# A decoder layer's expert activations: gates and transposed lists of a token tile made in the last step of the tile in front

## What is computed

```python
s = jnp.einsum('thpd,hpkd->thpk', q, subkeys)
s_top, i_top = lax.top_k(s, 16)                       # per half
cand = s_top[:, :, 0, :, None] + s_top[:, :, 1, None, :]
g_s, g_i = lax.top_k(cand, 16)
e = jnp.take_along_axis(cand_idx, g_i, axis=-1)
g = jax.nn.softmax(g_s, axis=-1)
act = jax.nn.gelu(jnp.einsum('thed,td->the', u[e], xb))
y = jnp.einsum('the,thed->td', g * act, v[e])
```

## Time and profile before

| what | value |
|---|---|
| median of the runs shown | 2279.5 us |
| profiled execution | 2279.13 us, its span 2277.4 us |
| mean granted TensorE clock | 0.944 |
| busy: PE, DVE, ACT, POOL | 2058.1, 1646.1, 854.5, 983.0 us |
| column products begin, units begin, last column | 993, 1093, 1715 us |
| ScalarE's conversion of a column (L2336), mean | 1.051 us |

### The profile page before, as it was taken

How to read it: one execution, slowest core, us unless ns; L and a number is a source line. 1 busy time by engine, 2 the same in 40 slices (tenths; PEclk the granted TensorE clock), 3 DMA queues, 4 the chain that set the end, 5 groups by cost and what they waited for, 6 DMA issues and landing times.

```text
span 2277.4 us, 32421 instructions
## 1 busy us (share of the span) xinstructions
PE 2058.1 (90%) x10515; PEld 1660.1 (73%) x10515; DVE 1646.1 (72%) x2982; ACT 854.5 (38%) x1715; POOL 983.0 (43%) x855
## 2 busy tenths in 40 slices
PE   8998998678789879999899799969987999999997
PEld 7774576334346548889898699969986888888885
DVE  3563156865223434898899999998867889989988
ACT  1232021223202211134766476648753333333331
POOL 1000133333100000047788778967994455554440
PEclk9999899879899879999999999989999999999998
DMA  5333222998740222336798798878999999999992
GB/s 195 79 72 118 90 87 76 363 331 305 263 172 3 111 84 65 98 125 230 233 308 294 232 300 293 292 256 274 308 355 382 373 387 402 405 394 387 385 387 112
DMA packets 239937, 547.81 MB, mean 241 GB/s; under 512 B 22190, under 2 KB 122335, under 8 KB 238394
## 3 DMA queue, kind: packets, MB, share of 16 engines
q1 hardware_dynamic: 110714, 287.40, 35.8%
q0 software_dynamic: 60736, 208.40, 24.9%
q10 hardware_dynamic: 68352, 50.34, 6.7%
HBM read 485.58 MB, written 60.02 MB: 240 GB/s over the span
## 4 chain that ended last, share of the span: by engine, by line
PE 30%; DVE 21%; POOL 5%; issue 4%; DMA 2%; ACT 0%; SPq 0%; DVEq 0%; ACTq 0%; POOLq 0%
PE psum L2797 20%; DVE u_gather L2430 8%; PE psum L2082 5%; PE psum L2551 4%; DVE hT L2458 4%; POOL uL L2196 3%; POOL u_gather L2188 2%; DMA S<-activation_table 2%; DVE eq L1987 1%; PE psum L2073 1%; DVE vL L2739 1%; DVE eq L1990 1%; DVE cand L1965 1%; DVE i_first L1951 0%; DVE vecs L1991 0%
## 5 line engine op out<-in xcount | busy, mean ns | idle before, releaser
L2188 POOL DMA_INDIRECT u_gather<-in_u_rows,gather_ids x160 | 211.3, 1321 | 456.4 <-DVE gather_ids L1998 348.1
L2196 POOL TENSOR_TENSOR uL<-u_raw,uH 128x512 fp32r<-128x512 f32 x256 | 379.3, 1505 | 61.5 <-ACT uH L2114 36.2
L2551 PE MATMUL psum<-hH,uH 128*128 128x384 f32 x1024 | 357.2, 349 | 42.3 <-POOL uL L2196 42.2
L2551 PE MATMUL psum<-hH,uL 128*128 128x384 f32 x1024 | 348.5, 340 | 0.0
L2551 PE MATMUL psum<-hL,uH 128*128 128x384 f32 x1024 | 348.1, 340 | 0.0
L2659 POOL DMA_INDIRECT v_gather<-in_v_rows,idx_now x160 | 236.1, 1476 | 249.5 <-DVE y_sample L2748 153.0
L2430 DVE CUSTOM_DVE_ANT_0 u_gather<-u_gather,h 128x1024 f32<-128x1024 f32 x160 | 292.0, 1825 | 44.9 <-DMA u_gather<-in_u_rows,gather_ids 36.1
L2797 PE MATMUL psum<-vH,wH 128*128 128x512 f32 x768 | 301.6, 393 | 14.8 <-DVE wL L2741 14.7
L2797 PE MATMUL psum<-vH,wL 128*128 128x512 f32 x768 | 300.7, 392 | 0.0
L2797 PE MATMUL psum<-vL,wH 128*128 128x512 f32 x768 | 300.5, 391 | 0.0
L2551 PEld LDWEIGHTS psum<-hH,uH 128*128 128x128 f32 x1024 | 197.0, 192 | 50.6 <-POOL uL L2196 50.3
(11 more groups left out here) (503 smaller groups left out, 3454.9 us busy)
## 6 DMA issues: line engine op xcount, KB each, us to landing
u_raw<-in_uT SPq DMA_DIRECT2D x128, 512.0 KB
S<-in_v_rows SPq DMA_DIRECT2D x64, 512.0 KB
v_rest<-in_v_rows SPq DMA_DIRECT2D x64, 512.0 KB
activation_table<-acts ACTq DMA_DIRECT2D x128, 192.0 KB
gate_table<-Gtile ACTq DMA_DIRECT2D x48, 512.0 KB
S<-gate_table SPq DMA_DIRECT2D x16, 768.0 KB
S<-activation_table SPq DMA_DIRECT2D x16, 768.0 KB
G_rest<-gate_table SPq DMA_DIRECT2D x16, 768.0 KB
```

Source lines behind the costliest of these rows:

```text
L2188: c.nc.gpsimd.indirect_dma_start(c.ug[:, k % RG], None, c.A["u_rows"].rearrange("j i d -> (j i) d"), bass.IndirectOffsetOnAxis(ap=c.ids[:, ...
L2196: ins = c.nc.gpsimd.tensor_tensor(c.uL[:, n % RU, d], c.u[:, n % RAW, d], c.uH[:, n % RU, d].bitcast(F32), ALU.subtract)
L2551: ins = nc.tensor.matmul(column[n % 4][:, 0:ND], w[:, n % RU, d], x[:, d], start=m == 0, stop=m == len(parts) - 1)
```

## The change

For each tile after the first, `tile_pre` runs at the start of the last step of the tile in front, the exponential and the gates in that step's places 0 and 2, and the transposes (`slots_out`, split off `slots_in`) in place 3. ScalarE's three copies (`slots_in`) run at place 0 of the tile's step 0, and the units and routing parts of step 0 are taken in turn with columns and dots like those of the other steps. The routing of a tile is spread over 28 of the 32 slots (34 parts), that of tile 0 over 26 (17 parts). Two of the dot lists change, with the same sums. Transposes wait for the copies of the tile before, and the copies for the comparisons and gatings of the tile before, since both now come sooner.

```diff
--- before.py
+++ after.py
@@ -2152,7 +2152,7 @@
 TSTEP = P // (UNIT * U_STEP)
 LEAD = 4
 STEP_COLS = ((2, 1) * 4, (5, 5, 5, 5, 5, 5, 4, 4), (5,) * 8, (4, 3) * 4)
-STEP_DOTS = ((1, 1, 1, 0, 0, 2, 2, 2), (6,) * 7 + (5,), (7, 6, 6, 6) * 2, (6,) * 8)
+STEP_DOTS = ((1, 1, 1, 0, 0, 2, 2, 2), (6,) * 5 + (5, 5, 7), (6,) * 7 + (8,), (6,) * 8)
 TAIL_DOTS = (2, 1, 1, 1, 1, 0)
 RAW = 3
 RU = 4
@@ -2233,7 +2233,7 @@
             return c.res0[:, 2] if p == 0 else b.res[:, 2] if p < STILE else c.resS[:, 2]
-        def steps(columns, dot, tile_pre, gates_out, tile_gates, slots_in, unit, route, flush):
+        def steps(columns, dot, tile_pre, gates_out, tile_gates, slots_out, slots_in, unit, route, flush):
@@ -2244,9 +2244,11 @@
             for p in range(STILE):
                 for st in range(TSTEP):
                     nc_, nd = STEP_COLS[p][st], STEP_DOTS[p][st]
-                    routed, gates = st == (0 if p else 5), st == (0 if p else 7)
-                    if routed:
-                        tile_pre(p)
+                    next_tile = st == TSTEP - 1 and p + 1 < STILE
+                    if p == 0 and st == 5:
+                        tile_pre(0)
+                    if next_tile:
+                        tile_pre(p + 1)
                     for i in range(max(U_STEP, nc_, nd)):
                         if i < nc_:
                             columns(n)
@@ -2254,21 +2256,22 @@
                         if i < nd:
                             dot(k)
                             k += 1
-                        if routed and i == 0:
-                            gates_out(p)
-                        if gates and i == 1:
-                            tile_gates(p)
-                        if st == 0 and i == 4 and p:
+                        if p == 0 and (st, i) == (5, 0):
+                            gates_out(0)
+                        if p == 0 and (st, i) == (6, 1):
+                            tile_gates(0)
+                        if next_tile and i == 0:
+                            gates_out(p + 1)
+                        if next_tile and i == 2:
+                            tile_gates(p + 1)
+                        if next_tile and i == 3:
+                            slots_out(p + 1)
+                        if p and (st, i) == (0, 0):
                             slots_in(p)
-                        if st and i < U_STEP:
+                        if i < U_STEP:
                             if p:
                                 unit(p, st, i)
                             route(p, st, i)
-                    if st == 0:
-                        for i in range(U_STEP):
-                            route(p, st, i)
-                        for i in range(U_STEP if p else 0):
-                            unit(p, st, i)
             tile_pre(STILE)
             for i, more in enumerate(TAIL_DOTS):
                 columns(n)
@@ -2299,7 +2302,7 @@
                     if n >= RAW:
                         sp.wait_ge(u_split, n - RAW + 1)
                         sp.dma_start(u[:, n % RAW], A["uT"][n]).then_inc(u_in[n % RAW], 16)
-                steps(columns, *[nothing] * 8)
+                steps(columns, *[nothing] * 9)
                 sp.wait_ge(res_ready, STILE)
                 for j in range(2):
                     sp.dma_start(c.v_raw[j], A["v_rows"][j]).then_inc(c.v_in[j], 16)
@@ -2323,7 +2326,7 @@
                 def dot(k):
                     if k + 2 < NDOT:
                         gather_u(c, pool, k + 2)
-                steps(columns, dot, *[nothing] * 7)
+                steps(columns, dot, *[nothing] * 8)
             @block.scalar
             def _(act):
@@ -2351,6 +2354,9 @@
                 def slots_in(p):
                     act.wait_ge(res_mm, p)
+                    if p > 1:
+                        act.wait_ge(hot_ready, PUNIT * (p - 1))
+                        act.wait_ge(gated, PUNIT * (p - 1))
                     nc.scalar.activation(slot_g[0][:], bank[5][:, 2 * P:3 * P], ACT.Copy)
                     nc.scalar.activation(slot_g[1][:], bank[5][:, 2 * P:3 * P], ACT.Copy, scale=-1.0)
                     nc.scalar.activation(slot_ij.rearrange("p u q t -> p q u t"),
@@ -2410,7 +2416,7 @@
                     if i < STORES:
                         store(NTB - 1, i)
-                steps(columns, nothing, nothing, gates_out, nothing, slots_in, unit, nothing, flush)
+                steps(columns, nothing, nothing, gates_out, nothing, nothing, slots_in, unit, nothing, flush)
             @block.vector
             def _(dve):
@@ -2490,30 +2496,35 @@
                     elif i == 6:
                         router.rows_of(c.resS, 0, 2 * TOPK, c.ids[:, :, GS])
+                def rest_of_tile(p, k):
+                    if k < 12:
+                        h, part = k // 3, k % 3
+                    elif k == 12 or k == 29:
+                        spare_dot()
+                        router.convert(b.first, BATCH)
+                        return
+                    else:
+                        h, part = BATCH + (k - 13) // 4, (k - 13) % 4
+                    if k > 29:
+                        router.pick(BATCH + k - 30, b.res)
+                    elif part == 3:
+                        router.pick(h - BATCH, b.res)
+                    else:
+                        router.part(scores_of(p + 1, h), b.first, h, b.res, part)
+
                 def route(p, st, i):
                     if p == 0:
                         slot = st * U_STEP + i
-                        for k in range(slot * 17 // 32, (slot + 1) * 17 // 32):
+                        for k in range(min(17, slot * 17 // 26), min(17, (slot + 1) * 17 // 26)):
                             rest_of_first(k) if k < 9 else rest_of_second(k - 9)
                     elif p == STILE - 1:
                         rest_of_sample(st * U_STEP + i)
                     else:
-                        if st == 0 and i == 2:
-                            dve.wait_ge(res_mm, p)
-                        if i < 3:
-                            router.part(scores_of(p + 1, st), b.first, st, b.res, i)
-                        elif st % BATCH == BATCH - 1:
-                            spare_dot()
-                            router.convert(b.first, BATCH)
-                            if st == PH - 1:
-                                for h in range(BATCH, PH):
-                                    spare_dot()
-                                    router.pick(h, b.res)
-                                spare_dot()
-                        elif st >= BATCH:
-                            router.pick(st - BATCH, b.res)
-                        if st == PH - 1 and i == 2:
-                            router.pick(BATCH - 1, b.res)
+                        slot = st * U_STEP + i
+                        for k in range(min(34, slot * 34 // 28), min(34, (slot + 1) * 34 // 28)):
+                            if k == 2:
+                                dve.wait_ge(res_mm, p)
+                            rest_of_tile(p, k)
                 places = dots = 0
@@ -2532,7 +2543,7 @@
                     while dots + DOT_LAG <= k:
                         next_dot()
-                steps(nothing, dots_late, tile_pre, nothing, tile_gates, nothing, unit, route, nothing)
+                steps(nothing, dots_late, tile_pre, nothing, tile_gates, nothing, nothing, unit, route, nothing)
                 while dots < NDOT:
                     next_dot()
                 dve.wait_ge(c.dot_done, NDOT)
@@ -2552,8 +2563,10 @@
                                                stop=m == len(parts) - 1)
                     ins.then_inc(u_mm, 1)
-                def slots_in(p):
+                def slots_out(p):
                     pe.wait_ge(res_ready, p + 1)
+                    if p > 1:
+                        pe.wait_ge(slots_ready, p - 1)
                     for q in range(3):
                         ins = nc.tensor.transpose(bank[5][:, q * P:(q + 1) * P], b.res[:, q], c.ident[:])
                     ins.then_inc(res_mm, 1)
@@ -2568,7 +2581,7 @@
                                                hot[:, n % RH, q], hot[:, n % RH, UNIT + q], start=True, stop=True)
                     ins.then_inc(g_mm, 1)
-                steps(columns, nothing, nothing, nothing, nothing, slots_in, unit, nothing, nothing)
+                steps(columns, nothing, nothing, nothing, nothing, slots_out, nothing, unit, nothing, nothing)
```

## The result

The changed kernel takes 2297.4 us, the median of seven runs (2290.1 to 2302.9); the kernel before took 2278.4 us (2270.3 to 2282.9) beside it. The ratio is 1.0083, with the interval 1.0059 to 1.0107: slower by 0.6 to 1.1%, some 19 us. The time lies in the predicted range (2257 to 2301), but outside the forecast's own range (2272 to 2291), and the forecast case, no change, did not come.

What follows compares the result with a forecast made beforehand. VectorE was taken to bound tiles 1 and 2, with GpSimd carrying the chain from 1551 us on. 2279.1 - 10.3 + 7.8 + 13.8 - 5.0 = 2285.4, less 2 us, gave 2283 us; range 2257 to 2301.

Steps and rivals of the forecast that it cites:

- forecast case: Whole kernel: 2283 us, own range 2272 to 2291, "no change" meaning within 0.5% (11.4 us); chance 0.40.
- The bound: VectorE bounds tiles 1 and 2, busy 210.0 of 218 and 218.7 of 227 us; delay at tile 3's entry reaches the end.
- What goes and what comes at tile 1: VectorE's waits: 9.4 us go, 7.8 come (1.3 for the exponential, 6.5 for the lists); worth nothing, 0 +- 3 us.
- Tiles 2 and 3: At their changes VectorE waits 3.5 and 5.7 us for the exponential, 2.3 us each for copied lists: 13.8 us together.
- What the waits give back: While VectorE idles, GpSimd's subtractions run alone, so VectorE's instructions stretch less: 5 us back.
- The spread of the routing: 34 parts in 28 slots: nothing by VectorE's sum; change in stretching bounded at +-17 us and taken as nothing.
- The early units: Products starting with three or four columns still to do fill TensorE's holes, but VectorE sets the rate: nothing.
- The sum: At tile 3's entry: 2279.1 - 10.3 + 7.8 + 13.8 - 5.0 = 2285.4; 2 us off before GpSimd's run gives 2283.
- The signs: VectorE idle 3 to 6 us before gate sums, 2 to 7 before first comparisons; tile 3's last column ends 1715 to 1722.
- Rival 1: Tiles 1 and 2: work shared by VectorE and GpSimd is the bound; even mixing saves 21 us of stretching: 2262; chance 0.27.
- the rule's other half: On SBUF access: a VectorE instruction with a single SBUF input does not contend with GpSimd, so the search costs GpSimd nothing.
- Rival 2: At a tile's start ScalarE is shut in waiting for three comparisons, 3.6 to 5 us lost per change: 2297; chance 0.27.

Runs made afterwards that it cites:

- half_before: The kernel before with each dot taken over 512 of its 1024 elements, the other half of the sum left out: 2216.5 us, ratio 0.9738.
- late_units: The changed kernel with the four units of a tile's first step moved to the end of that step: ratio to the kernel before 1.0085.
- lead1: The changed kernel with ScalarE's gatings one unit ahead of the products in place of two: 2309.8 us, ratio to the kernel before 1.0137.
- spread_only: The kernel before with only the routing of tiles 1 and 2 spread over 28 slots; gates, transposes and units stay where they were: ratio 1.0089.
- spread_32: As spread_only, but with the 34 routing parts of a tile spread over all 32 slots: ratio to the kernel before 1.0043.
- late_both: The changed kernel with gates and transposes at the end of the last step and step 0's units at its end: ratio to the kernel before 1.0059.
- late_gates: The changed kernel with the next tile's gates and transposes at the end of the last step, behind its columns: ratio to the kernel before 1.0066.
- after_spare: The changed kernel with two spare dots ahead of the wait for the exponential and three ahead of that for the lists: ratio to before 1.0072.

## Why the prediction was in its range and its forecast case was not

*The bound.* Right in part. Lighter dots shorten the tiles (half_before), though that may be VectorE's own load or what it shares with GpSimd; and the entry of tile 3 fixes the end: 17.5 us there, 17.8 at the last column. But VectorE's idle time does not price a change by itself: late_units took 18.4 us of it for nothing.

*What goes and what comes at tile 1.* 9.4 us of idle time went, and 11.8 us came (5.09 and 6.67), where 7.8 were forecast. The lists took what was said (6.67 for 6.5), the exponential 3.8 us more. Its own time was right: the whole stage lies 2.9 us earlier, and it ended at 1061.9 in place of 1064.8. VectorE stood in front of it at 1056.8 in place of 1063.5, 3.8 us sooner beyond that shift: the preparation of tile 1, which I had only put two dots earlier, came sooner still, and the two dots behind it took 2.6 us in place of 3.5.

*Tiles 2 and 3.* Forecast: 3.5 and 2.3 us, 5.7 and 2.3 us. Measured: 1.26 and 5.42, 7.94 and 8.57 us, 23.2 in place of 13.8. The places and the releasers are right, lead1 confirms the reason given for the first kind, the lengths are not. ScalarE's rows at tile 3 show why:

```profile
1492.65 0.69 ACT L2394 ACTIVATE hT<-hT,tri 128x128 f32<-128x128 f32 x2 [10.37 <-DVE hT L2464]
...
1497.00 0.68 ACT L2394 ACTIVATE hT<-hT,tri 128x128 f32<-128x128 f32 x2
...
1502.08 1.28 ACT L2353 ACT_TABLE_LOAD   x1 [0.40 <-ACT acts L2347]
1503.38 0.31 ACT L2353 ACTIVATE vecs<-vecs 128x128 f32<-128x128 f32 x1
...
1510.54 1.28 ACT L2347 ACT_TABLE_LOAD   x1
...
1524.96 1.06 ACT L2339 ACTIVATE uH<-u_raw 128x1024 fp32r<-128x1024 f32 x1 [2.49 <-DMA u_raw<-in_uT]
...
1527.46 0.39 ACT L2362 ACTIVATE bcol<-psum 128x256 f32<-128x256 f32 x1
```

VectorE's comparisons of units 28 and 29 stand beside them:

```profile
1491.67 0.95 DVE L2464 TENSOR_TENSOR hT<-iota,bcol 128x768 f32<-128x768 f32 x1
...
1493.68 0.95 DVE L2464 TENSOR_TENSOR hT<-iota,bcol 128x768 f32<-128x768 f32 x1
...
1494.55 1.22 DVE L2436 CUSTOM_DVE_ANT_0 u_gather<-u_gather,h 128x1024 f32<-128x1024 f32 x1
```

From the comparison of unit 29 on (its end, 1494.63) I had 7.6 us to the end of the exponential (1503.69); it took 9.1. ScalarE had waited 10.37 us for the comparison of unit 28, and the next came only 2.0 us behind it. ScalarE was still at unit 28's gating, a column and an eviction, and began unit 29's gated rows at 1497.00. The dot that was to cover the wait took 1.2 us in place of 1.9. For the lists the sum had left out the table load with which ScalarE goes back from the exponential (1.28 us, at 1510.54), and a conversion waits 2.49 us for its raw rows. I had summed the durations of ScalarE's queue and taken it as caught up; at tile 3 it was not.

*What the waits give back.* Forecast 5 us, measured 8.2 us of VectorE's busy time (485.33 to 477.11). The kind was right, the size a little small.

*The spread of the routing: this step failed.* "By VectorE's sum it is nothing" and "take nothing". spread_only gives 1.0089 with this part alone, 20.1 us of the stage, just outside the bound of 17. The bound was for stretching, and stretching went the other way: VectorE's busy time fell by 9.9 us. The work of VectorE is the same, but its place is not. Before, its heavy load (last picks, conversion, spare dots) lies at the change, where VectorE otherwise stands before a round trip over ScalarE and TensorE; in 28 slots that cover is gone, and VectorE idles for 9.46, 5.53 and 13.71 us in front of the same instructions. spread_32 gives half of the loss back. My argument looked at what the parts cost and not at what they hid. That the lost cover is the reason for this half is an argument from where the idle time stands; the runs show the edit that costs the time. The whole change without this part was not run, so that the rest would be free by itself is not shown.

*The early units.* They do fill TensorE's holes (34.2 to 24.4 us). "VectorE sets the rate, so it waits elsewhere: nothing" came true: it waits for low parts in the tiles, where the row of the whole run went from 42.2 to 46.2 us. Beside spread_only the rest of the change is worth 2.6 us of the stage to the good, too little to be told from scatter with one execution of each.

*The sum.* It had 13.4 us too little of new idle time (4.0 at tile 1, 9.4 at tiles 2 and 3) and 3.2 us too little given back, and it left a part at nothing that, tried alone, costs as much as the whole. At the changes 24.7 us more of idle time, less 8.2 of busy time, is 16.5, near the stage's 17.5, so the sum closes as arithmetic. It closes for every kernel in which VectorE has the same instructions, and that is no proof of the cause: late_both removed most of the new idle time (21.8 of 25.2 us), and most of the loss stayed (12.8 of 17.5 us).

*The signs.* Of those named for the forecast, TensorE's waits for gated rows under 6 us each and the earlier units of tile 3 came. VectorE's waits lay partly outside their ranges (1.26 and 7.94 us for 3 to 6; 8.57 for 2 to 7), and the last column product starts at 1729.5 us, not by 1722.

*The rivals.* Rival 1, less stretching, came true as a busy time (8.2 us) and not as a shorter tile. The page "SBUF — State Buffer" of the Trainium skill, section "Who interferes with whom", led to it: a VectorE instruction with two SBUF inputs and a GpSimd instruction that reads SBUF shut each other out for the whole instruction. From this I took that the search should be mixed evenly with columns. The dots did fall, from 190.6 to 178.8 us, which agrees; the time rose by 0.83%, so my inference from the rule to the time was wrong. The prediction gave the rule's other half without its exception: the same section says that casts can take both ports and then contend too. The trace agrees. The casts of the conversions (L1981), with one input, take 0.23 us or 3.1 us each: of the four in tiles 1 and 2, two are long before and all four after.

Rival 2 named the side (2297, measured 2297.4) and not the mechanism: behind the start of tile 1 ScalarE waits for comparisons 0.30, 1.81, 2.27 and 1.00 us where that rival wanted over 10 (the one wait of 10.37 us is in the last step of tile 2, and late_both has it too), and late_units, which puts these comparisons together again, gains nothing. That its time was met is chance, and so is it that the time lies in a range whose upper end comes from that rival.

*Open.* Half of the loss goes with where the last parts of the routing stand. What remains has no single cause that a run here shows. spread_32 (+9.5 us) goes with 12.5 us more of VectorE's idle time and 7.4 more of TensorE's and hardly any more slow products; late_both (+12.8 us) goes with 3.4 us more of VectorE's idle time and 2.9 more of TensorE's, with longer comparisons and casts on VectorE and with 4.0 us more of slow products. How far the change's other parts matter beside the spread (late_gates and after_spare say some 4 to 5 us) is within the scatter of single executions. No kernel tried that does all the work beats the one before.

## What to carry to other kernels

A filler load may be worth what it hides: before work of a loaded engine is spread more evenly, look at which round trip it covers where it stands, and try that edit by itself. An idle sum that closes says where the time shows, not what causes it; take the idle time away once and see if the time follows. Where the stages in front scatter, compare lengths between two instructions that both kernels have.

## What the runs showed of the hardware

Idle time taken from VectorE came back as longer instructions: between after and late_both 21.8 us of it went, and the same instructions took 17.9 us more (477.11 to 495.04).

A hole of TensorE can cost more than its length. Behind the one of 4.63 us at 1064.00 the products from 1065.02 to 1067.25 start 0.31 or 0.32 us apart and then 0.17. The granted clock is 0.50 from 1064.00 to 1065.00 and 1.00 from 1067.40 on, its two levels of 1.2 and 2.4 GHz. Over the stage that is 15.4 us for 133 products before and 23.8 us for 193 after, although TensorE's idle time grew by only 3.5 us: the holes of over 1 us are smaller and more of them (16 with a mean of 3.24 us before, 21 with 2.70 us after).

The casts of the conversions (L1981) take either 0.19 to 0.28 us or 3.1 us, with nothing between in any of these traces. Of nine in a run, two are long before, five after and none in half_before.
